# Three edits to a fused decoder step: the down projection joins the block of the up projection, the state's decay moves to ScalarE, and ScalarE takes every dense copy beside the prompt's sparse attention

## The chip, the cores and the metric

The kernel runs on one core of one Trainium2 chip, as one program. The metric is the time of one execution in microseconds (us), as the device counts it; lower is better. All data are float32.

## The reference

One inference step of a decoder layer for a prompt of 1024 tokens and a sample group of 8 sequences with 4 new tokens each (1056 rows), with the same weights. Of the layer, these parts matter here:

```
def ssd_scan(x, dt, A, Bm, Cm, h0):            # B: state space mixer, chunks of 128 tokens
    ...
    def step(h, inp):
        s_c, dec = inp
        return h * dec[:, :, None, None] + s_c, h
    ...
def nsa_cmp_sel(q, qpos, kc, vc, ksb, vsb, slopes):   # A: compressed, selected (and window) attention
    ...
# the input projection feeds A, B, C and the gates; one output projection; cross-attention; then:
# ConvFFN: up-projection (1024 -> 2 x 2816), causal depthwise convolution of width 3,
#          silu(a) * b, down-projection (2816 -> 1024), RMSNorm, added to the residual.
# Outputs: y_prompt, y_sample and the new caches and states, ffn_conv (last rows before the convolution) too.
```

The step of the state between chunks is h * dec + s_c: the decay is the product, one factor for each head.

## The kernel before

The program is a row of blocks. In each block the five engines run their own instruction lists and meet by semaphores; at a block's end all of them wait for each other. Within a block, several lanes (generators of instructions) are merged: `together` gives each lane a start and a length in units of the block, and the merged order of their steps is the order on every engine. No scheduler changes it later.

**The dense lane** (class `Dense`, L294 and L298) is the input projection. It is cut into units of 8 matmuls that add up in one PSUM bank `d_ps`, and it runs beside every other lane of the mixer to fill TensorE (PE in the profile). A unit's result is copied to an SBUF buffer `d_ob` (L318) and stored by SyncE (SP). Units are numbered; `on_act` says which parity is copied by ScalarE (ACT); the other parity is VectorE's (DVE). In the block with the prompt's sparse attention it has only one bank, so that the first matmul of a unit waits for the copy of the unit before it (`one_bank=True`).

**The SSD block** (function `ssd`, about 1000 to 1233 us) has, for each of 8 chunks of the prompt, a front lane (convolution and gates: VectorE and GpSimd, POOL in the profile, each convolve their own columns, L1719 to L1725, with sigmoids on ScalarE) and a scan lane. In the scan, TensorE turns B and C (L1835), makes the decays (L1843), C times state (L1862, semaphore `yo_made`), the new state's summand (L1868, `st_made`) and the output (L1876). VectorE then multiplies `ssd_state` by the decay (L1933), adds the summand (L1935) and adds to `st_updated`, for which the turning of the next chunk waits.

**The sparse attention block** (function `nsa_prompt_lane`, about 1236 to 1672 us) has 32 steps, each with scores on TensorE (L700), bias and row maxima on VectorE (L822, L835), exponentials on ScalarE (L777), weights on VectorE (L849), turning of the probabilities on TensorE (L686) with copies shared by ScalarE and VectorE (L752, L754), and values (L719). GpSimd makes scaled bias tables for it (L880).

**The feed-forward part** has two blocks. `ffn_up` (to 2689 us) makes the up projection as 11 passes of two slots, 7 products of half size each with 2 halves (`P1 P2 P6 P7 P5 P3 P4`, L3390) from tokens `up_u_T`, sums `ffn_T`, weights `up_up_w` and their sums `ffn_S`; VectorE adds the results in `ffn_h` and convolves them in `ffn_c`; the gated rows land in `feed_g_T`. At its end 44 transposes (L3408) turn `ffn_last` into rows, ScalarE copies them to `up_u_T` (L3444), and SyncE stores them as ffn_conv. `project_down` (from 2690 us) then loads the down weights `down_w` (quarters B11, B21, B12, B22 of 2816 KB each, L3051) and makes 7 products of quarter size as well (`P1 P2 P5 P3 P6 P4 P7`; P1 is L3081, the others L3074). GpSimd's last work of the program is to clear semaphores (`clear`, L103).

## Time and profile before

| what | value |
|---|---|
| median of 3 runs | 2987.34 us (2979.53 to 2987.98) |
| the profiled execution, its own time | 2986.59 us |
| its span, first to last instruction | 2984.8 us |
| TensorE busy | 2825.6 us (95%) |
| VectorE, ScalarE, GpSimd busy | 1309.1 us (44%), 616.8 us (21%), 486.1 us (16%) |
| mean clock granted to TensorE | 0.973 of full speed |

Busy shares are means over the whole program; what bounds it is read block by block. Matmuls are pipelined, so the start of a row of them and the idle time that is printed before it say more than the duration of one. A float32 matmul of the 128x512 form leaves two records, so that 88 records are 44 matmuls; a transpose leaves one.

### The profile page before, as it was taken

How to read it: one execution, taken by the hardware profiler on the slowest of the kernel's cores; microseconds unless marked ns; L12 is line 12 of the kernel's file. 1: busy time of each engine (PE TensorE's matmuls, PEld its weight loads, DVE VectorE, ACT ScalarE, POOL GpSimd, SP SyncE). 2: the span in 40 equal slices, each digit the busy share in tenths (PEclk: the TensorE clock that was granted, in tenths of full speed). 3: DMA queues.
4: the chain of work that ended last, by engine and by line, in shares of the span. 5: the costliest groups of instructions: out<-in, count | busy, mean ns of one | idle time of the engine just before them, and what ended most of it. 6: DMA issues, size and time to landing. Idle time of an engine off the chain costs nothing. (4 is left out here: it accounts for less than half of the span.)

```text
span 2984.8 us, 42427 instructions
## 1 busy us (share of the span) xinstructions
PE 2825.6 (95%) x15048; PEld 1967.7 (66%) x15048; DVE 1309.1 (44%) x2971; ACT 616.8 (21%) x1521; POOL 486.1 (16%) x355
## 2 busy tenths in 40 slices
PE   8999999998999999899999799999899999999998
PEld 5777777766666655566666566555688888874443
DVE  3111123232642597265665344234566666661321
ACT  2111000001322244244444211244200000010010
POOL 1200100002420344100000100011233333320011
PEclk9999999999999999999999899899899999999999
DMA  7544264435992643531111553300234343405020
GB/s 198 132 87 92 61 195 128 133 102 163 267 275 87 181 153 110 185 90 42 44 37 51 181 165 130 127 29 29 80 118 147 105 145 107 147 16 171 2 85 28
DMA packets 343544, 345.07 MB, mean 116 GB/s; under 512 B 61001, under 2 KB 310025, under 8 KB 341982
## 3 DMA queue, kind: packets, MB, share of 16 engines
q1 hardware_dynamic: 298706, 259.32, 30.1%
q10 hardware_dynamic: 44662, 83.46, 8.6%
q8 instruction: 104, 1.70, 0.2%
q14 instruction: 72, 0.59, 0.1%
HBM read 289.37 MB, written 110.01 MB: 134 GB/s over the span
## 5 line engine op out<-in xcount | busy, mean ns | idle before, releaser
L294 PE MATMUL d_ps<-d_w,mixer_u_T 128*128 128x288 f32 (+2 forms) x2048 | 585.2, 434 | 18.4 <-PEq L145 10.3
L294 PEld LDWEIGHTS d_ps<-d_w,mixer_u_T 128*128 128x128 f32 x2048 | 384.2, 195 | 160.9 <-issue 39.4
L298 PE MATMUL d_ps<-mixer_u_T,d_w 128*128 128x352 f32 x1152 | 397.6, 480 | 20.8 <-DVE d_ob L318 11.3
L298 PEld LDWEIGHTS d_ps<-mixer_u_T,d_w 128*128 128x128 f32 x1152 | 207.3, 194 | 126.9 <-issue 38.1
L3390 PE MATMUL ffn_ps<-ffn_T,up_up_w 128*128 128x264 f32 x704 | 163.8, 386 | 0.0
L318 DVE COPY d_ob<-d_ps 128x288 f32<-128x288 f32 (+3 forms) x144 | 66.4, 462 | 218.0 <-PE d_ps L294 169.7
L3390 PE MATMUL ffn_ps<-up_u_T,ffn_S 128*128 128x264 f32 x672 | 156.4, 386 | 0.0
L3074 PE MATMUL down_Y<-down_w,feed_g_T 128*128 128x512 f32 x352 | 151.9, 593 | 0.0
L3390 PEld LDWEIGHTS ffn_ps<-ffn_T,up_up_w 128*128 128x128 f32 x704 | 133.8, 190 | 22.9
L3390 PE MATMUL ffn_ps<-up_u_T,up_up_w 128*128 128x264 f32 x640 | 145.7, 386 | 0.0
L2882 PE MATMUL mix_B<-gates_o_T,mix_wb 128*128 128x352 f32 x480 | 144.8, 465 | 0.0
L3390 PEld LDWEIGHTS ffn_ps<-up_u_T,ffn_S 128*128 128x128 f32 x672 | 127.7, 190 | 21.8
L3390 PEld LDWEIGHTS ffn_ps<-up_u_T,up_up_w 128*128 128x128 f32 x640 | 121.6, 190 | 20.8
L2882 PEld LDWEIGHTS mix_B<-gates_o_T,mix_wb 128*128 128x128 f32 x480 | 92.5, 193 | 51.9 <-issue 2.0
L1407 PE MATMUL cmp_H<-cmp_rows_T,cmp_w 128*128 128x254 f32 (+1 forms) x576 | 122.6, 373 | 0.0
L3449 DVE TENSOR_TENSOR ffn_h<-ffn_kept,ffn_ps 128x264 f32<-128x264 f32 (+2 forms) x216 | 74.5, 370 | 109.2 <-PE ffn_ps L3390 106.6
L3074 PEld LDWEIGHTS down_Y<-down_w,feed_g_T 128*128 128x128 f32 x352 | 66.7, 190 | 83.6 <-issue 83.6
L3520 DVE SCALAR_TENSOR_TENSOR ffn_c<-ffn_h,ffn_now,ffn_c 128x1072 f32<-128x1072 f32 x88 | 117.5, 1335 | 3.1
L822 DVE CUSTOM_DVE_ANT_0 nsap_probs<-nsap_S,nsap_scaled 128x512 f32<-128x512 f32 (+11 forms) x256 | 97.2, 438 | 46.4 <-PE nsap_S L700 46.4
L1407 PEld LDWEIGHTS cmp_H<-cmp_rows_T,cmp_w 128*128 128x128 f32 x576 | 106.9, 197 | 14.2
L777 ACT ACTIVATE nsap_probs<-nsap_probs,nsap_neg 128x640 f32<-128x640 f32 (+9 forms) x192 | 112.6, 591 | 6.3 <-DVE nsap_neg L836 6.3
L4032 PE MATMUL tail_ps_a<-feed_g_T 128*128 128x512 f32 x224 | 101.5, 594 | 0.0
(535 smaller groups left out, 3876.7 us busy)
## 6 DMA issues: line engine op xcount, KB each, us to landing
...
cmp_rows<-cache_nsa_kv SPq DMA_DIRECT2D x128, 128.0 KB
...
```

What stands on the lines that cost most here:

```text
L294: mm = pe.matmul(bank(u)[0:rows, 0:cols], self.u_T[:, k, r0:r0 + rows], self.view(i)[:, k, :], start=(k == 0), stop=(k == DK - 1))
L298: mm = pe.matmul(bank(u)[:, 0:cols], self.view(i)[:, k, x, :], self.u_T[:, k, c * third:(c + 1) * third], start=(k == 0), stop=(k == DK - 1))
L318: copy(self.ob[0:rows, u % ring, 0:cols], bank(u)[0:rows, 0:cols]).then_inc(self.copied[u % 2], 1)
L777: act.activation(x, x, ACT.Exp, scale=DH ** -0.5, bias=neg[:, s % 3, g, br:br + 1], accum_out=sums[:, s % 3, g, br:br + 1]).then_inc(exped, 1)
L822: mm = dve.tensor_tensor_reduce(probs[:, s % 3, g, p0:p0 + b - a], S[u % 2][g][:, col:col + b - a], scaled[:, r % 2, g, c0:c0 + b - a], 1. ...
L1407: mm = pe.matmul(H[s][:, :, 0:blocks], w1[:, s, l, :], rows_T[:, r0:r0 + (KVH - 1) * LP + 1:LP, j:j + blocks], start=(l == 0), stop=(l == ...
L2882: mm = pe.matmul(B[u % BANKS][:, 0:third], wb[:, s, k, :], o_T[:, k, c * third:(c + 1) * third], start=(k == lo), stop=(k == hi - 1))
L3074: mm = pe.matmul(bank[:, :], lhs[:, k, P * p:P * (p + 1)], rhs[:, k, :], start=(start and k == 0), stop=(k == KH - 1), skip_group_check=no ...
L3390: mm = pe.matmul(bank(p, x)[:, 0:quarter], weights[:, k, :], tokens[:, k, :], start=(k == 0), stop=(k == KH - 1))
L3449: dve.tensor_tensor(out, a, b, ALU.add).then_inc(summed, 1)
L3520: dve.scalar_tensor_tensor(out, row[:, k:k + conv], now[:, k, a:a + 1], out, ALU.mult, ALU.add).then_inc(convolved, 1)
L4032: mm = pe.matmul(acc(t)[:, 512 * h:512 * (h + 1)], mix_T[:, k, t * P:(t + 1) * P], w_out[:, k, 512 * h:512 * (h + 1)], start=(k == 0), sto ...
```

## The change

Three edits. (1) `project_down` is gone; its programs (`down_programs`) run behind those of the up projection in the same block. The weights go to memory that the up projection has given up: B11 and the first 5 rows of B21 to `up_u_T`, the rest, B12 and B22 to `ffn_room`, one tile that also holds what were T, S, h, c and kept. The sums of P1 use banks that are free by then. The first 8 of the 11 weight rows of P1 are multiplied ahead of the 44 transposes, the last 3 behind them. The rows of ffn_conv now lie where B22 goes, so B22 is loaded when they are stored. (2) The decay of the SSD state is done by four ScalarE instructions of 64 columns, one for each head, in the place of one VectorE instruction of 256; and the front lane starts 0.004 of the block later. (3) `on_act=(0, 1)`: beside the prompt's sparse attention ScalarE copies the odd dense units too.

The diff, cut to its core; the parts of `project_down` that are not shown moved into the new functions as they are.

The first three pieces are in `ssd` (ScalarE's chunk, VectorE's chunk, the lanes), the next in `down_programs`, then `feed_forward` by engine (SyncE, TensorE, ScalarE, VectorE, GpSimd), the last in `decoder_step`.

```
+            if not sample:
+                act.wait_ge(yo_made, n + 1)
+                act.wait_ge(st_updated, n)
+                for h in range(NH2):
+                    act.activation(v3(state[:, :], NH2)[:, h, :], v3(state[:, :], NH2)[:, h, :], ACT.Copy,
+                                   scale=cs(P, slot, "dec")[:, h:h + 1]).then_inc(decayed, 1)
             yield
...
                 dve.wait_ge(st_made, n + 1)
-                dve.tensor_tensor(v3(state[:, :], NH2), v3(state[:, :], NH2), wide(cs(P, slot, "dec"), SP), ALU.mult).then_inc(decayed, 1)
-                dve.wait_ge(decayed, n + 1)
+                dve.wait_ge(decayed, NH2 * (n + 1))
                 dve.tensor_tensor(state[:, :], state[:, :], TS[:, 256:512], ALU.add).then_inc(st_updated, 1)
...
-        together(nc, *beside, (constants_lane, 0.0, 0.03), (setup, 0.085, 0.085), (front, 0.158, 0.675), (scan, 0.22, 0.675), (last, 0.9, 0.08))
+        together(nc, *beside, (constants_lane, 0.0, 0.03), (setup, 0.085, 0.085), (front, 0.162, 0.675), (scan, 0.22, 0.675), (last, 0.9, 0.08))
...
-def project_down(nc, lhs_T, weight, gain_row, x_rows, out_rows, ident, rows_out):
+def down_programs(st, lhs_T, weight, gain_row, x_rows, out_rows, ident, banks, u_T, up_w, past, room, multiplied, last_copied, rows_out):
...
-    EARLY = 5
+    EARLY, BEFORE = 5, 8
...
-        cuts = dict(B11=[0, 1, 3, 6, KH], B21=[KH, KH + 5, FFK], B12=[0, KH], B22=[KH, FFK])
+    X = [banks[7], banks[0], banks[1], banks[2]]
+    Y = banks[3:7]
+    cuts = dict(B11=[0, 3, BEFORE, KH], B21=[0, EARLY, KH], B12=[0, KH], B22=[0, KH])
...
+    def early_sp(sp):
+        load_w(sp, "B11")
+        load_w(sp, "B21")
+        sp.dma_start(x_s, chunks(x_rows(SAMPLES))).then_inc(xs_in, 16)
+
+    def late_sp(sp):
+        sp.wait_ge(rows_out, 32)
+        load_w(sp, "B22")
...
+    def begin_pe(pe):
+        pe.wait_ge(multiplied, 2 + 2 * KH)
+        first_product(pe, 0, len(cuts["B11"]) - 2)
+
+    def rest_pe(pe):
...
+        first_product(pe, len(cuts["B11"]) - 2, len(cuts["B11"]) - 1)
+        pe.wait_ge(multiplied, ALL_GATED)
+        pe.wait_ge(last_copied, ROWS_COPIED)
...
+    def middle_sp(sp):
+        load_w(sp, "B12")
...
+                sp.wait_ge(product, n_of(NB // 2 - 1, 1, NP, after("P3", 1)))
+                early_sp(sp)
+                sp.wait_ge(product, n_of(NB // 2 - 1, 1, NP, after("P4", 1)))
+                sp.wait_ge(packed, 4 + 2 * (NB - 1))
+                sp.wait_ge(convolved, n_of(NB // 2 - 1, 0, 6, 18))
+                middle_sp(sp)
                 sp.wait_ge(last_copied, NB // 2)
                 sp.dma_start(outs["ffn_conv_prompt"][0, 0], last_rows[0:pad, :]).then_inc(rows_out, 16)
                 sp.dma_start(outs["ffn_conv_sample"][0].rearrange("b r n -> (b r) n"), last_rows[pad:tail, :]).then_inc(rows_out, 16)
+                late_sp(sp)
...
+                pe.wait_ge(summed, added(NB // 2 - 1, 1, "W 1"))
+                begin_pe(pe)
                 pe.wait_ge(packed, 4 + 2 * NB)
                 pe.wait_ge(summed, NA + NA * NB)
...
+                rest_pe(pe)
...
+                act.wait_ge(multiplied, 2 + 2 * NB)
                 for g in range(NB // 2):
                     act.wait_ge(last_turned, g + 1)
...
+                down_act(act)
...
+                dve.wait_ge(st_copied, 1 + NB)
+                down_dve(dve)
...
+                down_pool(pool)
...
-                    together(nc, (dense.lane(36, one_bank=True, turn=2), 0, 1), (nsa_prompt_lane(nc, own, ins, proj, kc_T, vc, oa_T, ident, dense, raw, raw_in, raw_count), 0.02, 0.98),
+                    together(nc, (dense.lane(36, on_act=(0, 1), one_bank=True, turn=2), 0, 1), (nsa_prompt_lane(nc, own, ins, proj, kc_T, vc, oa_T, ident, dense, raw, raw_in, raw_count), 0.02, 0.98),
```

`late_sp` goes on with the gains, the rows of x and the stores of y, and `rest_pe` with P2, the samples, P5, P3, P6, P4 and P7, both as `project_down` had them.

**TensorE at the seam of the two feed-forward blocks.** Before, behind the loop over the passes: the transposes, the end of one block and the start of the next (two branches), then P1 (44 matmuls on `down_X`), P2 (33 on `down_Y`) and the rest.

```order
L3408 MATMUL ffn_ps<-const_ident,ffn_last 18x128 x44
L3344 UNCONDITIONAL_BRANCH
L3070 UNCONDITIONAL_BRANCH
L3081 MATMUL down_X<-down_w,feed_g_T 128x512 x44
L3074 MATMUL down_Y<-down_w,feed_g_T 128x512 x33
```

With the change, at the same place; P1 is L3092 and P2 L3103.

```order
L3092 MATMUL ffn_ps<-up_u_T,feed_g_T 128x512 x32
L3453 MATMUL ffn_ps<-const_ident,ffn_last 18x128 x44
L3092 MATMUL ffn_ps<-up_u_T,feed_g_T 128x512 x12
L3103 MATMUL ffn_ps<-up_u_T,feed_g_T 128x512 x5
L3103 MATMUL ffn_ps<-ffn_room,feed_g_T 128x512 x6
```

The 32 matmuls moved ahead of the transposes, and no branch stands between. On GpSimd the clearing in the block of `project_down` (16 semaphores) is gone, and that at the program's end has 47 instead of 31.

**VectorE in one chunk of the SSD block.** Before:

```order
L1925 TENSOR_TENSOR ssd_E<-ssd_E,ssd_G 128x512 x2
L1927 TENSOR_TENSOR ssd_y<-ssd_G,ssd_cur 128x256 x2
L1799 TENSOR_TENSOR ssd_xs<-ssd_x,ssd_sg 128x512
L1804 TENSOR_TENSOR ssd_xdt<-ssd_xs,ssd_cur 128x512
L1805 TENSOR_TENSOR ssd_xw<-ssd_xs,ssd_cur 128x512
L1933 TENSOR_TENSOR ssd_state<-ssd_state,ssd_cur 128x256
L1935 TENSOR_TENSOR ssd_state<-ssd_state,ssd_TS 128x256
L318 COPY d_ob<-d_ps 128x352
L1939 TENSOR_TENSOR ssd_y<-ssd_y,ssd_Y 128x512
L1942 TENSOR_TENSOR ssd_y<-ssd_y,ssd_skip 128x512
```

With the change (7 lines further down in the file):

```order
L1932 TENSOR_TENSOR ssd_E<-ssd_E,ssd_G 128x512 x2
L1934 TENSOR_TENSOR ssd_y<-ssd_G,ssd_cur 128x256 x2
L1941 TENSOR_TENSOR ssd_state<-ssd_state,ssd_TS 128x256
L1800 TENSOR_TENSOR ssd_xs<-ssd_x,ssd_sg 128x512
L1805 TENSOR_TENSOR ssd_xdt<-ssd_xs,ssd_cur 128x512
L1806 TENSOR_TENSOR ssd_xw<-ssd_xs,ssd_cur 128x512
L319 COPY d_ob<-d_ps 128x352
L1945 TENSOR_TENSOR ssd_y<-ssd_y,ssd_Y 128x512
L1948 TENSOR_TENSOR ssd_y<-ssd_y,ssd_skip 128x512
```

The product is gone, and the sum moved ahead of the three front instructions. On ScalarE the four new instructions stand behind the eight exponentials of the chunk (L1887) and ahead of the front's sigmoids.

**ScalarE at an odd dense unit in the sparse attention block.** Before:

```order
L752 COPY nsap_probs_T<-nsap_T 128x512
L550 DMA out_dil_sample<-cache_dil_w 16x3968 x2
L752 COPY nsap_probs_T<-nsap_T 128x512
L790 COPY nsap_oa<-d_ps 128x128
L777 ACTIVATE nsap_probs,nsap_sums<-nsap_probs,nsap_neg 128x512 x4
```

With the change:

```order
L753 COPY nsap_probs_T<-nsap_T 128x512
L551 DMA out_dil_sample<-cache_dil_w 16x3968
L319 COPY d_ob<-d_ps 128x352
L551 DMA out_dil_sample<-cache_dil_w 16x3968
L753 COPY nsap_probs_T<-nsap_T 128x512
```

The copy of the odd unit stands between two copies of turned probabilities, ahead of the exponentials of that step, as the copies of the even units do.

## Rows read from the trace of the kernel before

**Rows 1.** Busy us by stretch: PE, PEld, DVE, ACT, POOL, clock, DMA share, GB/s.

```profile
1036.00:1183.00 147.00, 134.35 (x631) 88.48 (x631) 129.91 (x169) 67.22 (x136) 66.17 (x49) 0.99 0.43 137
1262.00:1672.00 410.00, 391.12 (x2786) 259.58 (x2782) 244.24 (x943) 173.91 (x523) 13.47 (x4) 0.98 0.18 51
```

**Rows 2.** Waits, 1020 to 1185 us: waiting, waited for, us, times, longest.

```profile
PE ssd_TS L1835 <- DVE ssd_state L1935: 11.5, 7, 2.7
```

**Rows 3.** Timeline of one SSD chunk (start, us, engine, line), then the last chunk.

```profile
1090.48 0.65 PE L1868 MATMUL ssd_TS<-ssd_xw,ssd_bc 128*64 128x256 f32 x4
1092.75 0.74 DVE L1927 TENSOR_TENSOR ssd_y<-ssd_G,ssd_cur 128x256 f32<-128x256 f32 x2
1096.30 2.79 POOL L1719 TENSOR_TENSOR ssd_x<-ssd_x,ssd_cw 128x1024 f32<-128x1024 f32 x1
1096.81 2.56 DVE L1933 TENSOR_TENSOR ssd_state<-ssd_state,ssd_cur 128x256 f32<-128x256 f32 x1
1099.17 1.33 POOL L1721 TENSOR_TENSOR ssd_x<-ssd_x 128x512 f32<-128x512 f32 x1
1099.41 0.42 DVE L1935 TENSOR_TENSOR ssd_state<-ssd_state,ssd_TS 128x256 f32<-128x256 f32 x1
1100.89 0.96 DVE L1942 TENSOR_TENSOR ssd_y<-ssd_y,ssd_skip 128x512 f32<-128x512 f32 x1
...
1180.51 0.41 DVE L1933 TENSOR_TENSOR ssd_state<-ssd_state,ssd_cur 128x256 f32<-128x256 f32 x1
```

**Rows 4.** Groups by form, ScalarE, 1262 to 1672 us: count, busy us, mean ns.

```profile
L777 ACT ACTIVATE nsap_probs<-nsap_probs,nsap_neg 128x63 f32<-128x63 f32 x8 | 2.7, 336 | 0.0
```

**Rows 5.** Waits: TensorE 1240 to 1700 us, ScalarE 1262 to 1672 us.

```profile
PE d_ps L298 <- DVE d_ob L318: 11.0, 11, 3.4
ACT d_ob L318 <- PE d_ps L298: 54.2, 15, 5.9
```

**Rows 6.** Timeline, sparse attention block; in brackets idle time before it and its releaser.

```profile
1266.12 2.72 PE L298 MATMUL d_ps<-mixer_u_T,d_w 128*128 128x352 f32 x4 [3.43 <-DVE d_ob L318]
1345.38 1.09 PE L686 MATMUL nsap_T<-const_ident,nsap_probs 128*128 128x128 f32 x8 [2.24 <-DVE nsap_probs_T L754]
1442.77 3.27 DVE L835 TENSOR_SCALAR nsap_neg<-nsap_tops 128x4 f32<-128x4 f32 x1
1446.31 2.69 PE L298 MATMUL d_ps<-mixer_u_T,d_w 128*128 128x352 f32 x4 [3.27 <-DVE d_ob L318]
1461.01 0.45 ACT L318 COPY d_ob<-d_ps 128x352 f32<-128x352 f32 x1 [5.41 <-PE d_ps L298]
1474.25 0.53 DVE L318 COPY d_ob<-d_ps 128x352 f32<-128x352 f32 x1 [2.14 <-PE d_ps L298]
```

**Rows 7.** Timeline, end of the up projection: P3, P4, the first 16 transposes.

```profile
2670.30 3.72 PE L3390 MATMUL ffn_ps<-up_u_T,ffn_S 128*128 128x264 f32 x16
2673.86 3.72 PE L3390 MATMUL ffn_ps<-ffn_T,up_up_w 128*128 128x264 f32 x16
2678.53 1.92 PE L3408 MATMUL ffn_ps<-const_ident,ffn_last 128*18 128x128 f32 x16 [0.95 <-POOL ffn_last L3581]
```

**Rows 8.** The chain that ended last, in order of time: start, us, what.

```profile
2695.34 39.61 PE down_X L3081 x88
...
2858.30 37.77 PE down_X L3074 x88
```

**Rows 9.** DMA issues, 2685 to 2730 us: count, KB each, us to landing.

```profile
down_w<-ffn_w_down SPq DMA_DIRECT2D x1, 768.0 KB, 6.9
down_w<-ffn_w_down SPq DMA_DIRECT2D x1, 256.0 KB, 4.8
```

**Rows 10.** Busy us by stretch, columns of rows 1: behind a wait, weights streaming, the end.

```profile
1345.40:1350.00 4.60, 4.60 (x44) 4.08 (x46) 1.80 (x13) 4.60 (x10) 3.23 (x1) 0.66 0.00 1
...
2699.00:2702.00 3.00, 3.00 (x8) 1.33 (x7) 0.00 (x0) 0.00 (x0) 0.00 (x0) 1.00 1.02 388
...
2982.00:2985.00 3.00, 0.00 (x0) 0.00 (x0) 0.00 (x0) 0.00 (x0) 0.00 (x0) 0.50 0.01 3
```

More of the change, by code:

```diff
@@ L11 @@
 from contextlib import ExitStack
+from itertools import accumulate
 import numpy as np
@@ L2981, in project_down @@
     n = len(OUTS_IN_ORDER)
+    ALL_GATED, ROWS_COPIED = 2 + 2 * FFK, FFK // 2
     def after(m, p=PAIRS - 1):
         return ORDER.index((m, p)) + 1
[L2986 to L3236 removed]
@@ new lines, in down_programs, with B @@
+    c11, c12, c2 = st.sem("c11"), st.sem("c12"), st.sem("c21_c22")
+    squared, meaned, rooted, inverted = st.sem("squared"), st.sem("meaned"), st.sem("rooted"), st.sem("inverted")
+    scaled, added, stored = st.sem("scaled"), st.sem("added"), st.sem("stored")
+    w_k = weight.rearrange("(k p) n -> p k n", p=P)
+    sample_bank, first_y = Y[3], 1
+    def B(name, k0=0, k1=KH):
+        k, rows = [piece for piece in quads[name] if piece[0] <= k0][-1]
+        return rows[:, k0 - k:k1 - k, :]
@@ new lines, in x_of, with y_of, halves, chunks @@
+    def x_of(t):
+        p = t % PAIRS
+        return A("A12", 2 * p, 2 * p + 2) if t < PAIRS else B("B22", 2 * p, 2 * p + 2)
+    def y_of(t):
+        return top[:, t] if t < PAIRS else bottom(t - PAIRS)
+    def halves(rows):
+        return rows.rearrange("t (a c) -> t a c", a=2)
+    def chunks(rows):
+        return rows.rearrange("t (c j) -> c t j", j=C)
+    def load_w(sp, b):
+        r, j = KH * (int(b[1]) - 1), HALF * (int(b[2]) - 1)
+        for i in range(len(cuts[b]) - 1):
+            k0, k1 = cuts[b][i], cuts[b][i + 1]
+            sp.dma_start(B(b, k0, k1), w_k[:, r + k0:r + k1, j:j + HALF]).then_inc(w_in[b, i], 16)
```

459 lines of the change are left out of this document (218 added, 241 removed).

## Prediction

> **What bounds the kernel now.** I read the busy time by stretch first, then the waits of TensorE in the two mixer blocks that the change touches, then the timeline at the seam of the two feed-forward blocks and the chain that ended last. TensorE is the engine that everything is packed around: in the middle of the SSD block it is busy 134.4 of 147 us, in the sparse attention block 391.1 of 410 us [rows 1]. So an edit can gain only what TensorE idles, and these idle times have names. In the SSD block 12.6 us are idle, of which 11.5 us are seven waits of the next chunk's turning for VectorE's `ssd_state` [rows 2]. In the attention block 18.9 us are idle, of which at most 11.0 us (in a slightly wider stretch, eleven waits) are for VectorE's copy of a dense unit [rows 5]. At the seam, P4, the up projection's last product, ends at 2673.86 + 3.72 = 2677.58 us [rows 7], and the down projection's first matmul starts at 2695.34 [rows 8]: 17.8 us in which only the transposes are done. From there the chain that ended last stays on TensorE without a wait until its last product, so what is gained at the seam reaches the end.
>
> **Edit 1, the seam.** Before, from the end of P4 to the end of P1 it is 2695.34 + 39.61 - 2677.58 = 57.4 us [rows 7, 8]. With the change SyncE starts the weights when P3 is done, at 2670.30 + 3.72 = 2674.0 [rows 7]. The first piece is 768 KB. Its landing is bounded by the 4.8 us of the 256 KB piece that came first and the 6.9 us of the 768 KB piece that came behind two others [rows 9]; I take 4.8 us plus 512 KB more at the 388 GB/s at which weights stream [rows 10], 1.35 us, so 6.1 us and a start at 2680.2. TensorE waits 2.6 us. Every later piece streams faster than it is eaten (four matmul pairs, 3.4 us, for each 256 KB). The product at full clock takes 37.8 us, as a later one of the same size does [rows 8]; the 39.6 us of P1 had its first matmuls at half clock behind the long gap. The transposes take 44 x 1.92 / 16 = 5.3 us [rows 7]; ScalarE's copies run with them. A wait of 2.2 us was followed by a stretch at the lower clock (0.66 granted, 1.2 GHz for part of it) [rows 6, 10], and the four matmuls behind the 3.27 us wait took 2.69 us, where the pace of rows 8 scaled to their width, 4 x 0.43 x 352 / 512, makes 1.2 us [rows 6, 8]; for such a stretch I add 1.7 us. So P1 ends at 2680.2 + 37.8 + 5.3 + 1.7 = 2725.0, and 2734.95 - 2725.0 = 9.9 us are gained. Against it stand 16 more semaphores cleared at the very end. The trace does not record them; the last bytes had landed by 2982, and 31 of them and the end of the program fit into the rest, 2.8 us [rows 10], so 16 cost from nothing to 1.5 us; I take 0.9, nearer to the upper end since little else is known to stand there. Edit 1 gives 9.0 us; with the bounds (landing 4.8 us and no loss of clock; landing 6.9 us, 3.4 us of clock and 1.5 us of clears) 6.1 to 13.1.
>
> What hides the rest: B22 is now loaded only when the ffn_conv rows are stored, about 2720, and 2816 KB take 7.4 us at 388 GB/s [rows 10] and a landing of some 3 us; the samples need it behind P2, at 2725 + 28.3 = 2753. Without that cover each us of delay would be a us of time. Behind SyncE's early waits nothing else is queued. ScalarE now waits for the last gate before it copies rows, but TensorE comes to the transposes 27 us later.
>
> **Edit 2, the decay.** VectorE's product took 2.56 us in seven chunks and 0.41 us in the last [rows 3]: in the seven it ran beside GpSimd's multiplication of 2.79 us and ended just behind it. It goes, and the sum behind it moves ahead of the front's three instructions, from 1099.41 to about 1093.5 (the end of L1927, 1092.75 + 0.74) [rows 3]. The summand is there (L1868 ended at 1091.1 [rows 3]). So the turning gets its state some 6 us earlier, and the seven waits go, if VectorE can hold the faster pace: it is busy 129.9 of 147 us [rows 1], so the loop of a chunk (21 us) is its loop. It saves 0.4 us for certain; of the other 2.15 us a part comes back, because `y + skip` (L1942), also on two SBUF operands, is now what meets GpSimd's multiplication: it can start at 1099.1 instead of 1100.89, 1.8 us earlier, and the next instruction may lose up to 0.6 us to GpSimd's second step (1.33 us, of which about half is left by then) [rows 3]. That is 1.2 to 1.8 us for each chunk, against 1.64 us that TensorE waited. I take 1.5 us, seven times, less 0.5 for the ends: 10 us. Bounds: 7 x 0.41 = 2.9 us if the whole stall comes back; all 12.6 us of idle time and 1.7 us of clock, 14.3.
>
> The price of a form as narrow as the new ScalarE instruction is 0.34 us (128x63) [rows 4], four of them 1.3 us a chunk. ScalarE is busy 67.2 of 147 us [rows 1], and its next work, the sigmoids, waits for VectorE's convolution anyway, so I cost it at nothing; without that cover it would be 1.3 us a chunk, 10 us in all. The shift of the front lane by 0.004 of some 250 us only settles that order.
>
> By the Trainium skill (SBUF — State Buffer, "SBUF: two separate sides") a VectorE instruction with two SBUF inputs and a GpSimd instruction that reads SBUF exclude each other for a whole instruction. The trace agrees: 2.56 us beside, 0.41 us alone [rows 3]. By that rule alone the lost 2.15 us are not VectorE's own and could all move to the next such instruction; that is rival A below. Its page VectorE: DVE Perf Modes ("The TRN2 errata") speaks against the split as well: 224 cycles at 1.2 GHz for every ScalarE instruction on SBUF make four of 64 columns an estimated 0.96 us, more than the one instruction that they replace. The rows say the same, and it costs nothing only while ScalarE idles.
>
> **Edit 3, the odd copies.** The eleven waits are two long ones, 3.43 and 3.27 us, and nine short ones, 4.3 us together [rows 5, 6]. At 1266 VectorE sat with the weights of the first step ahead of the copy; the weights need the exponentials, so ScalarE is free sooner than VectorE; no row gives by how much, and I take off half, 1.6 us. At 1446 VectorE stood 3.27 us in a small instruction beside GpSimd's table [rows 6]; the same stall a quarter earlier fell beside an even unit, and TensorE then waited 2.24 us for the next copy on VectorE [rows 6]. So this one shrinks from 3.27 to 2.24, by 1.0 us. Of the nine short ones the copy itself is 0.45 instead of 0.53 us [rows 6], 0.7 us in all, and where VectorE was late with it, all goes; ScalarE idled before 15 of its 16 even copies here, 54.2 us together [rows 5]. I take 2.4 of 4.3 us. Edit 3 gives 5 us, with 0.7 (only the faster copy) to 13 (all eleven waits and 2 us of clock) as bounds. The copies on ScalarE, 18 x 0.45 us, lie in its idle time.
>
> **The sum.** 9.0 + 10 + 5 = 24 us from the profiled execution's 2986.59 us: 2962.6 us. The median of the runs is 0.75 us above that execution, so I predict 2963 us.
>
> **The rivals.** A: GpSimd's stall moves whole to `y + skip` in each chunk. Edit 2 then gives 2.9 us and 1.3 us of slack once, 5.8 less than summed: 2969. For it speaks that VectorE is busy 88% of that stretch [rows 1]; against it that it would start L1942 earlier by less than the rows allow. B: in the attention block TensorE waits for VectorE's turned probabilities instead of the copies, as at 1345 [rows 6]; edit 3 gives about 1 us: 2967. C: nothing is gained at the seam, since the weights come late or the wait drops the clock for long; edit 1 gives 0: 2972. D, the other side: ScalarE becomes the bound in the attention block. There is one bank, so an odd copy behind a burst of exponentials holds TensorE for as long. The other edits give 19 us, and slower by 9 us needs 28 / 18 = 1.6 us for each of the 18 odd copies; at 2 us it would be 2986.6 - 19 + 36 = 3004. Against it, the copies stand ahead of the exponentials of their step, and ScalarE idled before the even ones [rows 5]. E: more than summed, as waits removed give the clock back: below 2957.
>
> **How the numbers follow.** 0.3% is 9 us and about what a measurement of this kernel can tell from no change, so faster means below 2978. My forecast (2957 to 2968) has 0.50, A 0.17, B 0.13, C 0.07, E 0.05, D 0.04, and 0.04 is left for gains that show nowhere. Faster: 0.50 + 0.17 + 0.13 + 0.05 + half of C = 0.89; same: the other half of C and the rest, 0.07; slower 0.04. All bounds together would give 2986.6 - 40.4 + 0.75 = 2947 and 2986.6 - 9.7 + 0.75 = 2978; ends of three edits seldom meet, so the range is 2950 to 2976.
>
> **What would show each step.** The first matmul of P1 some 2.6 us behind P4, P1 and the transposes without a wait, B22 landed 25 us ahead of the samples; no wait of L1835's successor for `ssd_state`, and the GpSimd multiplication's stall seen in L1942's successor; no copy of `d_ob` among TensorE's waits longer than 2 us in the attention block. Wrong would make it: a wait for ScalarE's decay or copies, TensorE's new waits for `ssd_E` or `nsap_probs_T`, or the two mixer blocks each as long as before.

## The result, and the profile after

The changed kernel takes 2953.07 us (median of 4 runs, 2945.21 to 2956.31) against 2987.62 us for the kernel before (4 runs beside them, 2979.53 to 2987.98). The ratio is 0.9892, with a 95% interval of 0.987 to 0.9913: faster by 34.5 us in the medians and by 32.3 us by the ratio. The forecast was 2963 us. The direction and, in the main, the mechanisms held; the gain is larger than summed, and the time lies where rival E stood (below 2957).

The profiled executions differ by less than the medians do: spans of 2984.8 and 2954.5 us, 30.3 us apart. Stage by stage, read from the first and last start of each stage's matmuls on TensorE:

| stage | before, us | after, us | change |
|---|---|---|---|
| start to the first `ssd_TS` | 1017.8 | 1017.1 | -0.7 |
| SSD block (`ssd_TS`, first to last) | 163.8 | 154.6 | -9.2 |
| to the first `nsap_S` | 77.7 | 74.8 | -2.9 |
| sparse attention (`nsap_S`, first to last) | 384.3 | 375.1 | -9.2 |
| to the end of the merge (`mix_B`) | 211.1 | 210.2 | -0.9 |
| tail and up projection, to the end of P4 | 822.9 | 827.9 | +5.0 |
| end of P4 to the end of P1, transposes in it | 57.4 | 44.2 | -13.2 |
| from there to the end of the span | 249.9 | 250.6 | +0.7 |

The first, fifth and sixth rows hold nothing that the change touches. The 5.0 us lost in the tail are most likely the clock's and not the change's. Of the twelve further kernels below ten took 822.5 to 824.8 us for that stage, e1, e8 and e12 with the changed code there among them at 822.5 or 822.6; and e2, whose code there is that of the kernel before, took 827.8, e11 828.0. Busy us by stretch (the columns are those of [rows 1]), two stretches of that stage before and then after, with a clock of 0.91 twice, and then of 0.88 and 0.90:

```profile
1855.00:1955.00 100.00, 90.58 (x497) 56.24 (x497) 28.03 (x67) 25.79 (x61) 7.56 (x4) 0.91 0.32 104
...
2055.00:2155.00 100.00, 86.02 (x394) 59.71 (x393) 49.40 (x86) 36.17 (x76) 19.55 (x12) 0.91 0.13 50
```

```profile
1832.00:1932.00 100.00, 90.60 (x490) 57.16 (x490) 26.48 (x64) 25.55 (x60) 7.56 (x4) 0.88 0.32 104
...
2032.00:2132.00 100.00, 84.47 (x400) 57.41 (x399) 47.64 (x79) 37.49 (x79) 21.75 (x12) 0.90 0.10 40
```

Without this loss the profiles would be 35 us apart, about what the medians say.

**The seam.** Timeline of TensorE in the changed kernel, from P3 (start, us, engine, line; in brackets the idle time before it and its releaser):

```profile
2652.45 3.72 PE L3433 MATMUL ffn_ps<-up_u_T,ffn_room 128*128 128x264 f32 x16
2656.01 3.72 PE L3433 MATMUL ffn_ps<-ffn_room,up_up_w 128*128 128x264 f32 x16
2661.13 27.70 PE L3092 MATMUL ffn_ps<-up_u_T,feed_g_T 128*128 128x512 f32 x64 [1.40 <-DMA up_u_T<-ffn_w_down]
2688.67 4.97 PE L3453 MATMUL ffn_ps<-const_ident,ffn_last 128*18 128x128 f32 x44
2693.48 10.46 PE L3092 MATMUL ffn_ps<-up_u_T,feed_g_T 128*128 128x512 f32 x24
```

The chain that ended last, in the same place:

```profile
2656.20 4.80 DMA up_u_T<-ffn_w_down
...
2688.84 4.80 PE ffn_ps L3453 x44
2693.64 10.30 PE ffn_ps L3092 x24
2703.94 28.32 PE ffn_ps L3103 x66
```

P4 ends at 2656.01 + 3.72 = 2659.73. The first 768 KB land 4.80 us after their issue at 2656.20, and TensorE waits 1.40 us; before, 17.8 us lay between P4 and P1, with nothing but the transposes in them [rows 7, 8]. The product keeps its pace from the first matmul (27.70 + 10.30 = 38.0 us for the 88 matmuls, which took 39.61 [rows 8]), and there is no wait between its two halves and the transposes. B22 is issued at 2699.90, the weights have stopped streaming by 2711, and the samples that need it start at 2732.20: some 21 us of room, where the prediction had 25.

**The SSD block.** Timeline of one chunk of the changed kernel, VectorE and GpSimd:

```profile
1088.04 0.41 DVE L1941 TENSOR_TENSOR ssd_state<-ssd_state,ssd_TS 128x256 f32<-128x256 f32 x1
...
1092.02 2.80 POOL L1720 TENSOR_TENSOR ssd_x<-ssd_x,ssd_cw 128x1024 f32<-128x1024 f32 x1
...
1093.52 1.85 DVE L1948 TENSOR_TENSOR ssd_y<-ssd_y,ssd_skip 128x512 f32<-128x512 f32 x1
...
1094.90 1.59 POOL L1722 TENSOR_TENSOR ssd_x<-ssd_x 128x512 f32<-128x512 f32 x1
...
1095.40 1.64 DVE L1951 TENSOR_TENSOR ssd_y<-ssd_y,ssd_z 128x512 f32<-128x512 f32 x1
```

Groups by form on VectorE, 1018 to 1185 us (count, busy us, mean ns), first before and then after:

```profile
L1933 DVE TENSOR_TENSOR ssd_state<-ssd_state,ssd_cur 128x256 f32<-128x256 f32 x8 | 18.3, 2292 | 0.0
L1945 DVE TENSOR_TENSOR ssd_y<-ssd_y,ssd_z 128x512 f32<-128x512 f32 x8 | 8.4, 1048 | 0.3
L1725 DVE TENSOR_TENSOR ssd_x<-ssd_x,ssd_cb 128x512 f32<-128x512 f32 x7 | 7.0, 1002 | 0.2
L1942 DVE TENSOR_TENSOR ssd_y<-ssd_y,ssd_skip 128x512 f32<-128x512 f32 x8 | 6.1, 759 | 0.3
```

```profile
L1948 DVE TENSOR_TENSOR ssd_y<-ssd_y,ssd_skip 128x512 f32<-128x512 f32 x8 | 14.9, 1862 | 0.3
L1951 DVE TENSOR_TENSOR ssd_y<-ssd_y,ssd_z 128x512 f32<-128x512 f32 x8 | 12.2, 1520 | 0.3
L1726 DVE TENSOR_TENSOR ssd_x<-ssd_x,ssd_cb 128x512 f32<-128x512 f32 x7 | 4.8, 692 | 0.2
L1941 DVE TENSOR_TENSOR ssd_state<-ssd_state,ssd_TS 128x256 f32<-128x256 f32 x8 | 3.3, 408 | 0.0
```

The product's 18.3 us are gone. In the chunk shown `y + skip` ends at 1095.37, 0.55 us behind GpSimd's multiplication (1092.02 + 2.80 = 1094.82), and the next instruction ends 0.55 us behind GpSimd's next one. So part of the stall moved: `y + skip` costs 8.8 us more in the block and `y * z` 3.8 more, while L1726 costs 2.2 less. The waits of TensorE, 1018 to 1185 us, are one row in place of [rows 2]:

```profile
PE d_ps L299 <- DVE d_ob L319: 5.0, 2, 2.8
```

The clock granted over the block is 0.99 in both profiles, so these 9.2 us are not the clock's.

**The sparse attention.** Waits of TensorE in the changed kernel, 1250 to 1672 us:

```profile
PE d_ps L720 <- DVE nsap_probs_T L755: 5.5, 4, 1.4
PE d_ps L299 <- ACT d_ob L319: 4.3, 3, 3.7
PE nsap_T L687 <- DVE nsap_probs_T L755: 3.6, 2, 1.9
```

The 11.0 us of waits for a copy in [rows 5] are 4.3 us, and a single long one is left, 3.66 us at 1253.59 at the block's start. There the copy stands behind a burst of exponentials on ScalarE, which had itself waited 4.91 us for VectorE's `nsap_neg`. In e8 and e12, whose instructions in this block are the same, the longest is 1.9 and 1.7 us.

Within 1250 to 1672 us the three kinds of wait shown were 10.8, 5.5 and 2.2 us before (for a copy of `d_ob`, and for turned probabilities at L719 and at L686), 18.5 in all, and are 13.4 now. So the waits are 5.1 us less and the block is 9.2 us shorter. The granted clock of the block rose from 0.98 to 1.00, which fits the other 4.1 us.

### The profile page after: what moved, and what is told of

It is laid out like the page before. It is cut to its first block and busy times, and to the rows that moved or that the text cites. A ratio compares the mean times of both kernels' runs of the same rounds, so it can differ in the third digit from the quotient of the medians.

```text
span 2954.5 us, 42458 instructions
## 1 busy us (share of the span) xinstructions
PE 2814.6 (95%) x15048; PEld 1963.0 (66%) x15048; DVE 1294.8 (44%) x2945; ACT 631.4 (21%) x1571; POOL 485.6 (16%) x355
## 5 line engine op out<-in xcount | busy, mean ns | idle before, releaser
L295 PE MATMUL d_ps<-d_w,mixer_u_T 128*128 128x288 f32 (+2 forms) x2048 | 580.4, 431 | 18.4 <-PEq L146 10.3
L299 PEld LDWEIGHTS d_ps<-mixer_u_T,d_w 128*128 128x128 f32 x1152 | 205.5, 193 | 122.5 <-issue 32.3
L3497 DVE TENSOR_TENSOR ffn_room<-ffn_room,ffn_ps 128x264 f32<-128x264 f32 (+2 forms) x344 | 123.4, 391 | 191.0 <-PE ffn_ps L3433 188.3
L3433 PE MATMUL ffn_ps<-ffn_room,up_up_w 128*128 128x264 f32 x704 | 163.8, 386 | 0.0
L3433 PE MATMUL ffn_ps<-up_u_T,ffn_room 128*128 128x264 f32 x672 | 156.4, 386 | 0.0
L3103 PE MATMUL ffn_ps<-ffn_room,feed_g_T 128*128 128x512 f32 x360 | 156.0, 592 | 0.0
L319 DVE COPY d_ob<-d_ps 128x288 f32<-128x288 f32 (+6 forms) x126 | 57.0, 454 | 210.0 <-PE d_ps L295 164.3
L3433 PEld LDWEIGHTS ffn_ps<-ffn_room,up_up_w 128*128 128x128 f32 x704 | 133.8, 190 | 22.9
L3433 PEld LDWEIGHTS ffn_ps<-up_u_T,ffn_room 128*128 128x128 f32 x672 | 127.7, 190 | 21.8
L3103 PEld LDWEIGHTS ffn_ps<-ffn_room,feed_g_T 128*128 128x128 f32 x360 | 68.3, 190 | 85.6 <-issue 85.6
L3568 DVE SCALAR_TENSOR_TENSOR ffn_room<-ffn_room,ffn_now 128x1072 f32<-128x1072 f32 x88 | 117.5, 1335 | 3.1
L319 ACT COPY d_ob<-d_ps 128x352 f32<-128x352 f32 (+4 forms) x90 | 38.9, 432 | 310.6 <-PE d_ps L295 165.7
```

The lines of the kernel that those rows point to most:

```text
L295: mm = pe.matmul(bank(u)[0:rows, 0:cols], self.u_T[:, k, r0:r0 + rows], self.view(i)[:, k, :], start=(k == 0), stop=(k == DK - 1))
L299: mm = pe.matmul(bank(u)[:, 0:cols], self.view(i)[:, k, x, :], self.u_T[:, k, c * third:(c + 1) * third], start=(k == 0), stop=(k == DK - 1))
L319: copy(self.ob[0:rows, u % ring, 0:cols], bank(u)[0:rows, 0:cols]).then_inc(self.copied[u % 2], 1)
L3103: mm = pe.matmul(bank[:, :], lhs[:, k, P * p:P * (p + 1)], B(rhs, k, k + 1)[:, 0, :], start=(start and k == 0), stop=(k == KH - 1), skip_g ...
L3433: mm = pe.matmul(bank(p, x)[:, 0:quarter], weights[:, k, :], tokens[:, k, :], start=(k == 0), stop=(k == KH - 1))
L3497: dve.tensor_tensor(out, a, b, ALU.add).then_inc(summed, 1)
```

## The experiments

Twelve kernels were run. Where a line with a ratio stands, it is to the kernel before on the same chip, with its 95% interval; where none does, there was one execution, and the block lengths are those of its profile. Edits are cut to the words and lines that matter. Lengths of stages that a kernel does not touch say how far one profile can be trusted. Up to the SSD block they range from 1008.4 to 1022.1 us. The SSD block with unchanged code is 163.7 or 163.8 us in five of five, but that of the changed kernel is 154.6 us in it and in e8 and 157.5 in e12, instruction for instruction the same there; and the attention block of the changed kernel ranges from 371.6 (e12) to 376.2 us (e11).

Much of this is the granted clock. Over the SSD block it is 0.99 in the kernel before, e1, e3, e9, e10, the changed kernel and e8, 0.97 in e2, e4 and e12, and 1.00 in e5, e6, e7 and e11. The same code took 154.6 us at 0.99 and 157.5 at 0.97, an estimated 1.5 us for each hundredth, so block lengths are compared below with this beside them.

### One edit at a time: e1 to e4

e1 is the changed kernel with these lines back at the kernel before's:

```diff
...
-                for h in range(NH2):
-                    act.activation(v3(state[:, :], NH2)[:, h, :], v3(state[:, :], NH2)[:, h, :], ACT.Copy,
-                                   scale=cs(P, slot, "dec")[:, h:h + 1]).then_inc(decayed, 1)
...
+                dve.tensor_tensor(v3(state[:, :], NH2), v3(state[:, :], NH2), wide(cs(P, slot, "dec"), SP), ALU.mult).then_inc(decayed, 1)
...
-        (front, 0.162, 0.675)
-    dense.lane(36, on_act=(0, 1), one_bank=True, turn=2)
+        (front, 0.158, 0.675)
+    dense.lane(36, one_bank=True, turn=2)
```

> The kernel before with edit 1 alone (one block for both projections). Theory (the two traces set side by side, stage by stage): the seam is worth 13 us by itself, since the first 768 KB land in 4.8 us and the clock stays up: ratio 0.9956. Rival (the sum as predicted): 9 us, 0.9970, and what was gained above the sum is clock that other stages gave back. In both, the stretch from P4's end to P1's end shows it: 44 us or 47.5 us instead of 57.4.

2972.55 us, ratio 0.9951 (0.9932 to 0.9971), 14.6 us. From P4's end (2668.86) to P1's end (2713.10) it is 44.2 us, the theory's number:

```profile
2665.14 3.72 PE L3428 MATMUL ffn_ps<-ffn_room,up_up_w 128*128 128x264 f32 x16
2670.29 27.70 PE L3087 MATMUL ffn_ps<-up_u_T,feed_g_T 128*128 128x512 f32 x64 [1.43 <-DMA up_u_T<-ffn_w_down]
...
2702.64 10.46 PE L3087 MATMUL ffn_ps<-up_u_T,feed_g_T 128*128 128x512 f32 x24
```

e2 is the kernel before with the decay on ScalarE and the shift:

```diff
...
+                for h in range(NH2):
+                    act.activation(v3(state[:, :], NH2)[:, h, :], v3(state[:, :], NH2)[:, h, :], ACT.Copy,
+                                   scale=cs(P, slot, "dec")[:, h:h + 1]).then_inc(decayed, 1)
...
-                dve.tensor_tensor(v3(state[:, :], NH2), v3(state[:, :], NH2), wide(cs(P, slot, "dec"), SP), ALU.mult).then_inc(decayed, 1)
...
-        (front, 0.158, 0.675)
+        (front, 0.162, 0.675)
```

> The kernel before with edit 2 alone (decay on ScalarE and the front lane's start at 0.162). Theory: about half of GpSimd's stall comes back in y + skip and y * z, 1.2 us a chunk are left and seven waits for ssd_state are gone: 9 to 12 us, ratio 0.996 to 0.997. Rival A of the prediction (the stall moves whole): 4 us, 0.9986. Rival 2: the gain needs the changed attention block behind it, then it is less than 9 us here.

2975.49 us, ratio 0.9959 (0.9941 to 0.9978), 12.2 us; rival A's 0.9986 is outside. In its profile the block is 157.5 us, 6.3 shorter, with `y + skip` at 1825 ns as in the changed kernel. It differs from the changed kernel's 154.6 by the clock for the most part (0.97 against 0.99): behind the same wait of 2.80 us the same eight matmuls took 5.06 us here, and 2.63 in the changed kernel. TensorE in e2 and then in the changed kernel:

```profile
1138.02 5.06 PE L298 MATMUL d_ps<-mixer_u_T,d_w 128*128 128x352 f32 x8 [2.80 <-DVE d_ob L318]
```

```profile
1139.66 2.63 PE L299 MATMUL d_ps<-mixer_u_T,d_w 128*128 128x352 f32 x8 [2.80 <-DVE d_ob L319]
```

e12, with the changed kernel's instructions here, has the wait at 2.79 us and the eight matmuls at 5.06, so the difference is one between executions and not between kernels.

e3 is the kernel before with the odd copies on ScalarE:

```diff
-    dense.lane(36, one_bank=True, turn=2)
+    dense.lane(36, on_act=(0, 1), one_bank=True, turn=2)
```

> The kernel before with edit 3 alone (odd copies of the attention block on ScalarE). Theory from the two traces: 9 us, ratio 0.9969. Rival (as predicted): 5 us, 0.9983, and the other 4 us came with another start of that block behind a faster SSD block. The first and last score matmuls of the block show it: 375 us apart by the theory, 379 by the rival, 384 before.

2976.05 us, ratio 0.997 (0.9952 to 0.9988), 9.0 us, and 374.6 us from the first to the last `nsap_S`. The theory's numbers; the other start of the block played no part. Waits of TensorE in e3, 1250 to 1672 us:

```profile
PE d_ps L719 <- DVE nsap_probs_T L754: 5.4, 4, 1.4
PE nsap_T L686 <- DVE nsap_probs_T L754: 3.6, 2, 1.9
PE d_ps L298 <- ACT d_ob L318: 2.3, 3, 1.7
```

The waits for a copy fell by 10.8 - 2.3 = 8.5 us in that stretch and those for turned probabilities rose by 1.4. The net is 7.1 of the 9.7 us by which the block is shorter; the rest is clock. The four matmuls behind the long wait at the start took 2.72 us before [rows 6] and 1.45 here, and the granted clock of the block's first 200 us is 0.95 and 0.98 before, 0.97 and 1.00 here.

The three together are 14.6 + 12.2 + 9.0 = 35.8 us by their ratios, against 32.3 for the changed kernel by its ratio (26 to 39 by its interval) and 34.5 by the medians: they add, within what the runs can tell.

e4 is the shift alone:

```diff
-        (front, 0.158, 0.675)
+        (front, 0.162, 0.675)
```

> The kernel before with nothing but the front lane's start at 0.162 instead of 0.158, so that VectorE makes the state (product and sum) ahead of the next chunk's ssd_xs, ssd_xdt and ssd_xw, and not behind them. Theory: the product still costs its 0.41 to 2.56 us on an engine that is busy 88% of the stretch; TensorE's wait for ssd_state goes but a wait for later work on VectorE takes its place, so 0 to 3 us: ratio 0.999 to 1.000. Rival: the order was all of edit 2, and this alone gives the same 9 us as e2 (0.997).

2984.19 us, ratio 0.9982 (0.997 to 0.9995): 5.4 us by the ratio, 2.4 by the medians and 2.5 in the block's length (161.3). That is more than the theory's 0 to 3 in the first and inside it in the others, and less than the rival's 9. The block's waits of TensorE fell by more than its length, from 12.5 us (11.5 for `ssd_state`, 0.7 for `ssd_E`, 0.3 for a copy) to 7.6, while the granted clock was 0.97 and not 0.99; so the order alone is worth something, 2.4 to 5.4 us by these measures. Groups by form and then the waits of TensorE, both 1018 to 1185 us, in e4:

```profile
L1942 DVE TENSOR_TENSOR ssd_y<-ssd_y,ssd_skip 128x512 f32<-128x512 f32 x8 | 15.2, 1897 | 0.3
L1933 DVE TENSOR_TENSOR ssd_state<-ssd_state,ssd_cur 128x256 f32<-128x256 f32 x8 | 6.5, 812 | 0.0
```

```profile
PE d_ps L298 <- DVE d_ob L318: 5.2, 3, 2.6
PE ssd_Y L1876 <- DVE ssd_E L1925: 2.4, 2, 1.4
```

The product fell from 2292 to 812 ns just by standing elsewhere, and `y + skip` rose to 1897. The stall is GpSimd's, and goes to whoever stands beside it.

### The decay and the stall: e5 and e6

e5 is e2 without the shift:

```diff
-        (front, 0.162, 0.675)
+        (front, 0.158, 0.675)
```

> The kernel before with the decay on ScalarE but the front lane's start left at 0.158, so that VectorE's sum stays behind ssd_xs, ssd_xdt and ssd_xw. Theory: the sum has one operand in PSUM and took 0.41 us whatever GpSimd did, so it ends 2.2 us a chunk earlier than before, TensorE's waits for ssd_state (0.5 to 2.7 us) all but go, and y + skip stalls as it does in e2: the SSD block is 157 to 160 us instead of 163.8, ratio 0.996 to 0.998. Rival: the shift is what takes the waits away; then the seven waits are still seen and the ratio is 0.999 or more.

2974.64 us, ratio 0.9964 (0.995 to 0.9978), 10.8 us. The block is 153.2 us, shorter than the theory's 157 to 160, and no wait for `ssd_state` is seen. The clock was 1.00 there against 0.97 in e2, so the 4.3 us between these two blocks say nothing for or against the shift. But the shift, which by the prediction "only settles that order", is not needed for the gain. From its timeline:

```profile
1082.09 2.81 POOL L1719 TENSOR_TENSOR ssd_x<-ssd_x,ssd_cw 128x1024 f32<-128x1024 f32 x1
1082.60 0.41 DVE L1940 TENSOR_TENSOR ssd_state<-ssd_state,ssd_TS 128x256 f32<-128x256 f32 x1
...
1084.07 1.37 DVE L1947 TENSOR_TENSOR ssd_y<-ssd_y,ssd_skip 128x512 f32<-128x512 f32 x1
```

The sum starts and ends inside GpSimd's multiplication and takes its 0.41 us all the same; it reads one operand from PSUM. `y + skip`, both operands in SBUF, ends 0.54 us behind the multiplication (1085.44 against 1084.90).

e6 is the changed kernel with GpSimd's multiplication by the taps cut to one column; the other 255 go on unmultiplied, so its outputs are not the layer's:

```diff
-            eng.tensor_tensor(x, x, cw[0:m, :, c0:c1], ALU.mult).then_inc(sem, 1)
+            c = c0 + 1 if c0 else c1
+            eng.tensor_tensor(x4[0:m, slot, :, c0:c], x4[0:m, slot, :, c0:c], cw[0:m, :, c0:c], ALU.mult).then_inc(sem, 1)
```

> The changed kernel with GpSimd's multiplication of the convolution's taps cut from 256 columns to one (the other columns go on unmultiplied). Theory (the stall belongs to whichever two-operand VectorE instruction meets that multiplication): y + skip falls from 1.86 us to the 0.7 us that it takes alone, y * z from 1.52 to between 0.7 and 1.1, in all 1.2 to 2 us a chunk, and the SSD block ends some us sooner (waits for d_ob of 5.0 us smaller). Rival: y + skip is slow for its place (right behind the PSUM sum), not for GpSimd: it stays at 1.8.

2942.15 us in one execution. The block is 147.3 us, 7.3 shorter, without one wait of TensorE on another engine in it; those waits were 5.0 us, and the clock is 1.00 instead of 0.99. Groups by form on VectorE, 1012 to 1180 us, in e6:

```profile
L1949 DVE TENSOR_TENSOR ssd_y<-ssd_y,ssd_skip 128x512 f32<-128x512 f32 x8 | 9.6, 1198 | 0.3
L1952 DVE TENSOR_TENSOR ssd_y<-ssd_y,ssd_z 128x512 f32<-128x512 f32 x8 | 8.4, 1047 | 0.3
```

`y + skip` is 0.66 us faster and `y * z` 0.47, in all 1.13 us a chunk, just under the 1.2 to 2 of the theory. It is slow for GpSimd, not for its place. It does not fall to 0.7 because GpSimd's additions stall it too: in each of the seven chunks that have one beside it, it ends 0.55 us behind GpSimd's first addition.

### Copies in the SSD block: e7

e7 is the changed kernel with the same edit at the dense units beside the SSD block:

```diff
-    dense.lane(36, settle=False)
+    dense.lane(36, on_act=(0, 1), settle=False)
```

> The changed kernel with the SSD block's odd copies on ScalarE too, as edit 3 did for the attention block. Theory: the two waits for VectorE's d_ob (5.0 us, 2.8 the longest) shrink to about 1 us each, since ScalarE comes free of the normalization 0.9 us sooner than VectorE, and VectorE loses 18 copies of 0.52 us: the block is 150 to 153 us instead of 154.6 and the ratio to before 0.987 to 0.989. Rival: ScalarE's waits (for the exponentials' operands, for y) stand ahead of odd copies and TensorE waits for ScalarE instead: 155 to 160 us and 0.989 to 0.991.

2950.04 us, ratio 0.9878 (0.9855 to 0.9901); the block is 152.8 us. The waits for a copy fell from 5.0 to 3.3 us (three, 1.8 the longest), but two short ones for `ssd_E` (0.9 us) and one for GpSimd (1.0) came up, so that the waits are 5.2 us in all, as long as before. The block is shorter by 1.8 us, which the clock, 1.00 instead of 0.99, accounts for. The numbers are inside the theory, its reason is not borne out, and by the times e7 is not to be told from the changed kernel.

### The seam: e8 and e12

e8 is the changed kernel with a smaller first piece:

```diff
-    cuts = dict(B11=[0, 3, BEFORE, KH], B21=[0, EARLY, KH], B12=[0, KH], B22=[0, KH])
+    cuts = dict(B11=[0, 1, 3, BEFORE, KH], B21=[0, EARLY, KH], B12=[0, KH], B22=[0, KH])
```

> The changed kernel with one row of weights (256 KB) as the first piece at the seam, ahead of two rows (512 KB), instead of three rows at once. Theory: the landing of a first piece is 4.8 us whatever its size up to 768 KB, so P1 starts as late as with three rows (1.4 us behind P4's end) and the two pieces' issue costs nothing. Rival (the prediction's step): 512 KB less at 388 GB/s land 1.35 us sooner and the wait all but goes.

The theory fell. DMA issues of e8, 2654 to 2655.3 us (count, KB, us to landing), and of the changed kernel, 2655 to 2657:

```profile
up_u_T<-ffn_w_down SPq DMA_DIRECT2D x1, 512.0 KB, 4.5
up_u_T<-ffn_w_down SPq DMA_DIRECT2D x1, 256.0 KB, 2.6
```

```profile
up_u_T<-ffn_w_down SPq DMA_DIRECT2D x1, 1280.0 KB, 8.1
up_u_T<-ffn_w_down SPq DMA_DIRECT2D x1, 768.0 KB, 4.8
```

A first piece of 256 KB lands in 2.6 us, one of 768 KB in 4.8: 2.2 us for 512 KB more. TensorE no longer waits at the seam (P4 ends at 2658.42, and so begins P1), and from P4's end to P1's end it is 42.6 us instead of 44.2:

```profile
2658.42 27.47 PE ffn_ps L3092 x64
```

This is read from the chain of the profile alone; the one execution took 2953.4 us.

e12 is the changed kernel with the first loads issued when P4 is done:

```diff
-                sp.wait_ge(product, n_of(NB // 2 - 1, 1, NP, after("P3", 1)))
+                sp.wait_ge(product, n_of(NB // 2 - 1, 1, NP, after("P4", 1)))
                 early_sp(sp)
```

> The changed kernel with the down projection's first loads issued when P4 is done, not when P3 is. Theory (the seam's gain is loads that run under P4, and the clock needs no long wait to fall): the issue comes 3.7 us later, so TensorE waits 5.1 us instead of 1.4 and the first matmuls run at the lower clock for a while, 1.5 to 2 us more; from P4's end to P1's end it is 49 to 50 us instead of 44.2. Rival (the block boundary itself was the cost, the loads' time is nearly free): under 46 us.

The timeline of TensorE in e12, from P4:

```profile
2653.41 3.72 PE L3433 MATMUL ffn_ps<-ffn_room,up_up_w 128*128 128x264 f32 x16
2662.07 29.30 PE L3092 MATMUL ffn_ps<-up_u_T,feed_g_T 128*128 128x512 f32 x64 [4.93 <-DMA up_u_T<-ffn_w_down]
2691.21 4.97 PE L3453 MATMUL ffn_ps<-const_ident,ffn_last 128*18 128x128 f32 x44
2696.01 10.47 PE L3092 MATMUL ffn_ps<-up_u_T,feed_g_T 128*128 128x512 f32 x24
```

The one execution took 2958.84 us. From P4's end (2657.13) to P1's end (2706.48) it is 49.35 us, the theory's 49 to 50. The wait is 4.93 us, and the 64 matmuls behind it take 29.30 us instead of 27.70: the clock's price of a wait of that length is 1.6 us, and it was nothing behind the changed kernel's 1.40. So of the 13.2 us at the seam 5.2 are the issue under P4, with the clock that it saves; the other 8 come of one block without a boundary in it, and are not split further.

### Which copies: e9 and e10

e9 and e10 are the kernel before with `on_act=(1,)` and `on_act=()` in the attention block:

```diff
-    dense.lane(36, one_bank=True, turn=2)
+    dense.lane(36, on_act=(1,), one_bank=True, turn=2)
```

> The kernel before with the attention block's odd copies on ScalarE and its even ones on VectorE (the sides exchanged). Theory (it is where VectorE stands at a copy that costs, whichever side it is, and each engine is late at other places): the two long waits of 3.4 and 3.3 us shrink to some 1.7 us, but even copies on VectorE meet waits of their own, so the block is 378 to 384 us long against 384 before and 375 with all on ScalarE; ratio 0.998 to 1.000. Rival: only the odd places were bad, and the exchange alone gives the 9 us of e3: 375 us, 0.997.

> The kernel before with all copies of the attention block on VectorE, the opposite of edit 3. Theory: VectorE is busy 0.6 of that block and in long series of instructions, so TensorE waits for d_ob at even copies as it did at odd ones, another 8 to 12 us: the block is 392 to 396 us. Rival: half of the copies already meet every wait there is and the block stays within 3 us of 384.

e9: 2982.78 us, ratio 0.999 (0.9976 to 1.0004), but a block of 374.9 us; the profile speaks for the rival (only the odd places were bad), the times for the theory. The clock may be what divides them: over the block it is 1.00 here, 0.99 in e3 and 0.98 before, so a part of these 9 us is not the exchange's. How large a part stays open. Waits of TensorE in e9, 1230 to 1640 us:

```profile
PE d_ps L298 <- ACT d_ob L318: 2.3, 3, 1.7
PE d_ps L298 <- DVE d_ob L318: 1.1, 4, 0.4
```

The waits for ScalarE are those of e3, and even copies on VectorE cost only 1.1 us. e10: a block of 391.0 us, 6.7 longer, and 2994.06 us. Its waits for copies are 11.6 us in 14, hardly more than the 10.8 of before, so most of the loss is not in the waits that were expected; the granted clock from 1246 to 1650 us is 0.97 against 0.98 before, which may be some 4 us of it. Both expectations (392 to 396, and within 3 of 384) missed.

### All that helped: e11

The changed kernel with e7's and e8's lines and the shift taken back.

```diff
-        (front, 0.162, 0.675)
-    dense.lane(36, settle=False)
-    cuts = dict(B11=[0, 3, BEFORE, KH], B21=[0, EARLY, KH], B12=[0, KH], B22=[0, KH])
+        (front, 0.158, 0.675)
+    dense.lane(36, on_act=(0, 1), settle=False)
+    cuts = dict(B11=[0, 1, 3, BEFORE, KH], B21=[0, EARLY, KH], B12=[0, KH], B22=[0, KH])
```

> The changed kernel with three things that the earlier runs point to: the front lane's start back at 0.158 (153.2 us for the SSD block in e5 against 157.5 in e2), the SSD block's odd copies on ScalarE (e7) and one row as the first piece at the seam (e8). Theory (they add): SSD block 150 to 152 us, no wait at the seam, 2947 to 2950 us, ratio 0.987. Rival: with the sum late and the copies on ScalarE the two SSD changes cure the same waits, and it is e7's 0.9878 less the 1.4 us of the seam.

2955.24 us (2947.54 to 2962.49), ratio 0.9886 (0.9869 to 0.9903). The SSD block is 151.6 us, as the theory has it, and TensorE's waits for a copy there are 2.3 us; the seam has no wait. But the whole is no faster than the changed kernel or e7. By its profile it stood 5.0 us behind the changed kernel before the SSD block began, where no edit of it reaches, and lost 4.4 more between that block and the attention. So one execution varies by more than the 4 us that were to be had. The expected 2947 to 2950 us were missed, and no kernel here is shown to beat the changed one.

## Why the prediction was right, and where it was short

**Edit 1: 9.0 summed, 13.2 at the seam less 0.7 for the clears.** e1 gives it alone. The shape was right: first matmul soon behind P4, no wait behind it, the transposes 4.8 us (5.3 summed), B22 never late. Two terms were mis-sized. The landing was taken as 6.1 us and measured 4.80, which is the prediction's lower bound; and "a wait of 2.2 us was followed by a stretch at the lower clock" was carried over to this wait as 1.7 us, while the wait was 1.40 us and the clock did not fall. e12 shows that the term is real where the wait is long: 1.6 us behind 4.93. The clears were at most 0.7 us (the last row of the table), 0.9 summed. With 4.8 and 0 in place of 6.1 and 1.7 the sum gives 2734.95 - (2674.0 + 4.8 + 37.8 + 5.3) = 13.1 of the 13.2 us. The "landing of some 3 us" that the prediction gave B22 comes from no row; nothing hung on it, with 21 us of room.

**Edit 2: 10 summed, 9.2 in the block, 10.8 and 12.2 timed alone (e5, e2).** The step "it saves 0.4 us for certain; of the other 2.15 us a part comes back" is what happened: of the product's 18.3 us `y + skip` and `y * z` took 12.6 back in eight chunks, other instructions of VectorE, `ssd_xs` and L1726 for the most part, became 4.6 us shorter, and VectorE works 10.3 us less for the eight chunks, 1.3 us a chunk (9.3 less within the block as the table cuts it). The prediction named 1.2 to 1.8 and took 1.5. Two things were read too narrowly. Its sum let `y + skip` lose 0.76 us (2.56 less the 1.8 by which it starts earlier) and the next instruction up to 0.6; they lost 1.10 and 0.47, and what others gave back was in no term. And it held the earlier place of the sum to be the reason why the waits go, "so the turning gets its state some 6 us earlier"; e5, where the sum stays behind, gains as much within the intervals, and e4, where only the order changes, gains 2.4 to 5.4 us. What counts, by all that the profiles show, is how long VectorE's loop of a chunk is: in all fourteen kernels the block is 19.4 to 21.1 us longer than VectorE is busy in it, whether it is 147.4 us long (e6) or 163.7. In e6 TensorE is busy 147.3 of 147.4 us, so there its own work is the limit as well. The wait that was left turned into waits for `d_ob` copies, 5.0 us, which the prediction did not foresee; e7 shows that copies on ScalarE only exchange them for others. Another 2.9 us came between this block and the next, in no term of the sum. Of the eight kernels with the decay on ScalarE seven are 1.2 to 3.1 us shorter there and e11 is 1.5 longer, and e4 is unchanged; what makes it is not settled. The cost on ScalarE was hidden, as said: four instructions of 334 ns, 1.05 us a chunk (8.4 us for 32), with no wait of TensorE or VectorE for `ssd_state`. By the Trainium skill (VectorE: DVE Perf Modes, "The TRN2 errata") 224 cycles each come to an estimated 0.75 us for four at 1.2 GHz before any element is read, or 0.96 with 64 columns; the trace's 1.05 lies a little above it. By the Trainium skill (SBUF — State Buffer, "SBUF: two separate sides") a VectorE instruction with two inputs in SBUF and a GpSimd instruction that reads SBUF exclude each other. The trace agrees: the stalled instructions of 128x512 ended 0.54 or 0.55 us behind GpSimd's, the product of 128x256 ended 0.28 us behind, and the sum with one operand in PSUM was free of it.

**Edit 3: 5 summed, 9.2 in the block, 9.0 timed alone (e3).** This is the step that was furthest off in size. The long wait at 1266 was halved in the sum (1.6 off) and measured 1.66 left of 3.43 in e3, so right there. The one at 1446 was to shrink from 3.27 to 2.24; no wait for a copy stands there any more, but one of 1.68 us for turned probabilities. Of the nine short ones 2.4 us of 4.3 were taken, and all but 0.6 went. In e3 the waits are then 7.1 us less, net of 1.4 more for turned probabilities, and some 2.5 us of clock come on top. In the changed kernel the long wait at the start is 3.66 us and so was not shortened; its waits are 5.1 us less, which is what was summed, and 4.1 us are clock. The prediction counted clock only in its upper bound. Rival B (turned probabilities in place of the copies) came to 1.4 us; rival D (ScalarE late) showed in one place, the 3.66 us behind the exponentials, and not at each odd copy: the waits for ScalarE are 2.3 us in e3 and 4.3 with all three edits. So three things that the prediction named as signs against it were seen, though the forecast held: a wait for a copy longer than 2 us, a wait for ScalarE's copy, and a new wait for `nsap_probs_T`.

**The sum.** 24 us were summed. Against it stand 3.5 us more at the seam (12.5 with the clears), 2.1 more at and behind the SSD block (12.1) and 4.2 more in the attention block: 33.8 us, where the medians differ by 34.5, the ratio gives 32.3 and the three edits alone add to 35.8. The profiles' 30.3 us are these 33.8, 1.6 us of the untouched stages, less the 5.0 us of the tail. All three excesses lie inside the bounds that the prediction gave for its edits. Rival E's reason, clock given back, fits some 4.1 us in the attention block and the 1.7 us that the seam did not pay. Whether the waits removed gave the clock back is argued and not shown, since the clock of the same code differs between executions too. The rest are a landing that was priced too high and gains in no term of the sum. The chance of 0.05 for E was too small: three terms taken near the middle or below of wide bounds all came out above it or at it.
